# Two transformer blocks at batch 1: the first modulation columns in shift and scale pairs, with part of their sums on the tensor engine

## The chip, the core and the metric

The kernel runs on one core of one Trainium2 chip. The metric is device microseconds of one launch. Before the change three runs took 2953.93, 2954.15 and 2958.77 us; the median is 2954.15 us.

## The reference, cut to what matters

All arrays are float32. There are 256 positions and a width of 2048. A vector c modulates both norms of the first block:

```
mod = silu(c) @ w_ada + b_ada                      # w_ada 2048 x 12288
sh1, sc1, gt1, sh2, sc2, gt2 = split(mod, 6)
h = rmsnorm(x, g_mix) * (1 + sc1) + sh1
x = x + (1 + gt1) * mixer(h, w_in, w_a, w_b, w_o)  # h @ w_in comes first
h = rmsnorm(x, g_ffn) * (1 + sc2) + sh2
x = x + (1 + gt2) * conv_ffn(h, w_up, ..., w_down)
```

A second block follows: a gated convolution, then a squared-ReLU layer of width 8192. Every matrix is read once from memory, 554 MB in all. The change lies ahead of, and in the first steps of, `h @ w_in`.

## The kernel before, in words

**Pieces.** Every product against a matrix goes by pieces of 512 rows by 512 columns (1 MB). SP loads a piece into one of four `raw` buffers. ACT rounds it to `whi` (`split_hi`, L518), DVE makes the rest `wlo` (`split_lo`, L819), and both have two buffers. PE multiplies 16 blocks of it by three products each (L1310 to L1312), 48 matmuls in all (`piece`). The activations are held in two parts as well, `xh` and `xl`. A step t is one piece. ACT may write `whi` for piece t only when piece t-2 has been multiplied (`s_used`). The pieces of w_in are the steps from t = 0; four of them make one group of 512 output columns.

**The modulation.** w_ada has 24 groups of 512 columns, 4 MB each. The first 8 are sh1 (groups 0 to 3) and sc1 (groups 4 to 7) and are needed before any piece can be multiplied. SP loads each in four quarters into the buffers `ada_first`. DVE multiplies each of the 16 chunks of a group by its value of silu(c) and adds (`add_product`, L902 and L905), in two running sums (`first_sum`). PE then adds over the 128 partitions: in `modulation` (L1358) the sums are the stationary operand and a column of ones is the moving one, so a matmul has one column. A quarter's buffer is loaded anew when DVE has used its four chunks.

**The order at the start.** SP first issues 21 small vector loads, the constants and the positions, then the four quarters of group 0, then x. PE turns the vectors and x (L1383), and takes the mean of squares (`statistic`, L1349). DVE computes the rotary angles (L883 to L896), then the eight groups, then reads all eight out of PSUM at once (L921), makes `wlo` of pieces 0 and 1, the reciprocal root (`root`, L839 to L847), and normalises the 16 chunks of x (`norm_split`, L859 and L869). PE starts the pieces as soon as the first chunk is there.

**The background groups.** The other 16 groups of w_ada come in half pieces of 0.5 MB. Two buffers (`ada`) form a ring: POOL issues a load (L467) when DVE has used the half piece before the last in the same buffer. DVE takes them in `half_piece`, which stands in its program just ahead of each `split_lo`; the function `beside(t)` says how many belong to step t. They are 3 in two steps for t below 24, and some 1.1 per step after. DVE executes in order, so a half piece that has not landed holds the `split_lo` behind it. Steps from t = 24 add the attention of the mixer.

## Time and profile before

| | |
|---|---|
| profiled execution, span | 2955.1 us |
| median of the three runs | 2954.15 us |
| PE busy | 2716.0 us, 92% |
| DVE busy | 1836.5 us, 62% |
| ACT busy | 1227.9 us, 42% |
| read from memory | 553.45 MB, 188 GB/s over the span |

The profile gives the profiled execution by its span; nothing else is listed around it, and it lies 1 us above the median. PE is the busiest engine over the whole, but not in the first slices of the page, where DVE and the DMA are. So the start is read from the trace, in microseconds from its beginning.

### The profile page before, as it was taken

What the parts mean: (1) busy time and instruction counts of PE and PEld (TensorE: products, weight loads), DVE (VectorE), ACT (ScalarE), POOL (GpSimd) and SP (SyncE); (2) the same over time, 40 slices, a digit from 0 to 9 for tenths busy, and PEclk for the clock granted to TensorE, in tenths of its full rate; (3) what the DMA queues carried; (4) which work ended last, traced back from release to release, by engine and by line L of the source; (5) the groups of instructions that cost most, each with busy time, mean ns of one, the idle gap of its engine ahead of it and who ended that gap; (6) DMA issues with size and microseconds to landing.
All of it is one profiled execution on the core that took longest, in us unless ns stands there. A gap on an engine that the chain in (4) does not pass through costs nothing.

```text
span 2955.1 us, 51569 instructions
## 1 busy us (share of the span) xinstructions
PE 2716.0 (92%) x21611; PEld 2670.4 (90%) x21611; DVE 1836.5 (62%) x1881; ACT 1227.9 (42%) x1200; POOL 325.1 (11%) x364
## 2 busy tenths in 40 slices
PE   3499999999998999999999988777899999999998
PEld 3499999998998999999999977776899999999997
DVE  6966667775777555534565457999555544455444
ACT  1233643344433554432444346664443333333332
POOL 0011111100111000000000014885000000000000
PEclk8599999999999999999999999888999999999998
DMA  8888567754776455554555543332255555555552
GB/s 323 299 291 292 214 238 249 242 182 162 243 255 227 171 175 184 181 182 159 185 185 175 181 130 126 115 114 72 87 170 182 179 183 185 186 183 185 184 184 89
DMA packets 266602, 557.72 MB, mean 189 GB/s; under 512 B 11991, under 2 KB 13144, under 8 KB 266200
## 3 DMA queue, kind: packets, MB, share of 16 engines
q1 hardware_dynamic: 248023, 488.47, 48.8%
q0 software_dynamic: 18432, 67.12, 6.7%
q8 instruction: 114, 1.87, 0.3%
q14 instruction: 33, 0.26, 0.0%
HBM read 553.45 MB, written 2.10 MB: 188 GB/s over the span
## 4 chain that ended last, share of the span: by engine, by line
PE 76%; DVE 14%; issue 4%; DMA 3%; ACT 2%; SPq 1%; POOL 0%; DVEq 0%; ACTq 0%; POOLq 0%
PE ps L1310 22%; PE ps L1311 22%; PE ps L1312 22%; DVE ucv L1197 5%; DVE wlo L819 3%; DMA att<-in_w_ada 3%; DVE norm_rows L905 2%; PE ms L1312 1%; PE ms L1311 1%; PE ms L1310 1%; PE ms L1594 1%; PE ms L1349 1%; ACT whi L518 1%; PE ms L1345 1%; DMA att<-in_x 0%
## 5 line engine op out<-in xcount | busy, mean ns | idle before, releaser
L1310 PE MATMUL ps<-xh,whi 128*128 128x256 f32 x5136 | 1489.7, 290 | 113.3 <-DVE wlo L819 51.8
L819 DVE TENSOR_TENSOR wlo<-raw,whi 128x2048 fp32r<-128x2048 f32 x429 | 991.0, 2310 | 917.7 <-ACT whi L518 916.7
L1311 PE MATMUL ps<-xl,whi 128*128 128x256 f32 x5136 | 1474.3, 287 | 0.0
L1312 PE MATMUL ps<-xh,wlo 128*128 128x256 f32 x5136 | 1473.8, 287 | 0.0
L518 ACT CAST whi<-raw 128x2048 fp32r<-128x2048 f32 x429 | 816.5, 1903 | 1438.9 <-PE ps L1312 1291.3
L1310 PEld LDWEIGHTS ps<-xh,whi 128*128 128x128 f32 x5136 | 1006.8, 196 | 127.3 <-issue 71.5
L1311 PEld LDWEIGHTS ps<-xl,whi 128*128 128x128 f32 x5136 | 1006.7, 196 | 3.2 <-issue 2.9
L1312 PEld LDWEIGHTS ps<-xh,wlo 128*128 128x128 f32 x5136 | 1005.9, 196 | 0.0
L1312 PE MATMUL ps<-gh,wlo 128*128 128x256 f32 x1024 | 289.0, 282 | 0.0
L1310 PE MATMUL ps<-gh,whi 128*128 128x256 f32 x1024 | 288.9, 282 | 0.0
L1311 PE MATMUL ps<-gl,whi 128*128 128x256 f32 x1024 | 288.9, 282 | 0.0
L905 DVE SCALAR_TENSOR_TENSOR norm_rows<-att,cact,norm_rows 128x512 f32<-128x512 f32 x296 | 217.5, 749 | 60.2 <-DMA att<-in_w_ada 54.6
L1310 PEld LDWEIGHTS ps<-gh,whi 128*128 128x128 f32 x1024 | 193.2, 189 | 0.1
L1312 PEld LDWEIGHTS ps<-gh,wlo 128*128 128x128 f32 x1024 | 193.1, 189 | 0.0
L1311 PEld LDWEIGHTS ps<-gl,whi 128*128 128x128 f32 x1024 | 193.0, 188 | 0.1
L506 POOL TENSOR_TENSOR ucv<-ucv,prod 128x256 f32<-128x256 f32 x180 | 190.5, 1095 | 0.0
L467 POOL DMA_DIRECT2D att<-in_w_ada x128 | 92.8, 725 | 734.0 <-DVE norm_rows L905 520.0
L1197 DVE SCALAR_TENSOR_TENSOR ucv<-upad,cols,ucv 128x256 f32<-128x256 f32 x240 | 173.4, 794 | 0.0
L489 POOL TENSOR_TENSOR prod<-sq 128x256 f32<-128x256 f32 x24 | 20.7, 874 | 996.3 <-ACT sq L528 979.7
L721 ACT ACTIVATE prod<-upad,cols 128x256 f32<-128x256 f32 x180 | 87.0, 505 | 55.3 <-POOL ucv L506 53.0
L1310 PE MATMUL ps<-fh,whi 128*128 (+1 forms) x352 | 99.4, 282 | 3.5 <-DVE cb L1149 3.5
L1312 PE MATMUL ms<-fh,wlo 128*128 (+1 forms) x352 | 99.9, 284 | 0.0
(230 smaller groups left out, 2059.0 us busy)
## 6 DMA issues: line engine op xcount, KB each, us to landing
raw<-in_w_in SPq DMA_DIRECT2D x88, 1024.0 KB, 5.3
raw<-in_w_up SPq DMA_DIRECT2D x88, 1024.0 KB, 4.8
att<-in_w_ada POOLq DMA_DIRECT2D x128, 512.0 KB, 4.9
raw<-in_ffn_w_up SPq DMA_DIRECT2D x64, 1024.0 KB, 5.1
raw<-in_ffn_w_down SPq DMA_DIRECT2D x64, 1024.0 KB, 5.1
raw<-in_conv_w_pw SPq DMA_DIRECT2D x48, 1024.0 KB, 5.3
raw<-in_w_down SPq DMA_DIRECT2D x44, 1024.0 KB, 5.1
att<-in_w_ada SPq DMA_DIRECT2D x32, 1024.0 KB, 7.2
```

The costliest lines, as they stand in the source:

```text
L467: pool.dma_start(slots[m % 2][:, :, :], w_ada[m % 8][:, :, n:n + NCOL]).then_inc(s_adaland[m % 2], 16)
L506: nc.gpsimd.tensor_tensor(dst, dst, src, ALU.add).then_inc(s_padd, 1)
L518: nc.scalar.copy(whi[t % SPL][:, :, :], raw[t % RAW][:, :, :]).then_inc(s_hi, 1)
L721: nc.scalar.activation(dst, src, ACT.Copy, scale=w).then_inc(s_prod, 1)
L819: nc.vector.tensor_tensor(wlo[t % SPL][:, :, :], raw[t % RAW][:, :, :], whi[t % SPL][:, :, :].bitcast(F32), ALU.subtract).then_inc(s_lo, 1)
L905: ins = nc.vector.scalar_tensor_tensor(sums, w, cx, sums, ALU.mult, ALU.add)
L1197: nc.vector.scalar_tensor_tensor(ucv[:, c, :], src, w, ucv[:, c, :], ALU.mult, ALU.add).then_inc(s_dwd, 1)
L1310: mm(o, h, rh, start=start, stop=False, skip_group_check=True)
L1311: mm(o, h, rl, start=False, stop=False, skip_group_check=True)
L1312: return mm(o, l, rh, start=False, stop=stop, skip_group_check=True)
L1345: mm(o, mean_w[:, :], pair_sum(k, i), start=i == 0, stop=i == 7).then_inc(s_psum, 1)
L1349: ins = mm(o, mean_w[:, :], sq[:, 2 * (i % 2) + m, :], start=i == 0 and m == 0, stop=i == 7 and m == 1)
```

## The change

**Loads.** SP issues the constants, only the first three vectors (b_ada, c, g_mix), then group 0 and at once pieces 0 and 1 of w_in. Pieces 2 and 3 follow the third and fifth group. The other vectors, the positions and x are issued by ACT, ahead of its own work.

**Pairs.** The eight groups are taken in the order 0, 4, 1, 5, 2, 6, 3, 7 (`FIRST`), so that each pair gives shift and scale of four chunks of x. After a pair DVE normalises those four chunks (`norm_first`) and PE multiplies one piece of w_in with them.

**Sums.** Of a group's 16 chunks DVE does 10 (`first_products`). PE does the other 6: the chunk of w_ada is the stationary operand and silu(c) the moving one, 24 matmuls of one column (`first_modulation`), and then 8 more over DVE's two sums. The quarters 2 and 3 are reloaded only when PE has used them too.

**Background.** The angles move into the steps t = 4 to 12. The ring of half pieces starts after the last pair is normalised, and its first 36 half pieces belong to the steps 3 to 23 in place of 0 to 23. Steps 0 to 3 are now inside the loop over pairs.

```diff
+FIRST = [j + 4 * half for j in range(4) for half in range(2)]
+BY_VECTOR = 10
+BY_TENSOR = KC - BY_VECTOR // KC
+B_ANGLE = 4
...
-            return 3 * t // 2
+            return 36 * max(0, t - 3) // 21
...
-        first_sum = [mod_sum, [tCDE[:, 0:NCOL], tCDE[:, NCOL:2 * NCOL]]]
+        first_sum = [[ch(26, 28), ch(28, 30)], [tCDE[:, 0:NCOL], tCDE[:, NCOL:2 * NCOL]]]
...
+        first_vecs = [v for v in vec_parts if v[3] < P]
+        other_vecs = [v for v in vec_parts if v[3] >= P]
...
+            load_vectors(sp, first_vecs, s_vin[0])
...
+            for n, group in enumerate(FIRST):
                 for q in range(KC):
-                    sp.wait_ge(s_chain, g * DC + KC * (q + 1))
-                    sp.dma_start(ada_first[q][:, :, :], w_ada[q][:, :, bass.ds(g * NCOL, NCOL)]).then_inc(s_adaring[q], 16)
+                    if n:
+                        if KC * q < BY_VECTOR:
+                            sp.wait_ge(s_first, BY_VECTOR * (n - 1) + min(BY_VECTOR, KC * (q + 1)))
+                        if KC * (q + 1) > BY_VECTOR:
+                            sp.wait_ge(s_firstmm, BY_TENSOR * (n - 1) + q + 1 - (KC - BY_TENSOR))
+                    sp.dma_start(ada_first[q][:, :, :], w_ada[q][:, :, group * NCOL:(group + 1) * NCOL]).then_inc(s_adaring[q], 16)
+                for q in {0: (0, 1), 2: (2,), 4: (3,)}.get(n, ()):
+                    sp.dma_start(raw[q][:, :, :], blocks("w_in")[q][:, :, 0:NCOL]).then_inc(s_land[q], 16)
...
+            load_vectors(act, other_vecs, s_vin[1])
+            act.dma_start(posi, A["positions"]).then_inc(s_in[1], 16)
+            x_in = A["x"].rearrange("b (c p) (h t) -> p (b c) h t", p=P, t=T)
+            for c in range(2):
+                act.dma_start(att[:, 8 * c:8 * c + 8, :], x_in[:, c]).then_inc(s_in[2], 16)
+            act.wait_ge(s_trc, 1)
...
-            norm_hi(0, lambda c: mod[:, c:c + 1])
+            for j in range(4):
+                for c in range(4 * j, 4 * j + 4):
+                    act.wait_ge(s_nt, c + 1)
+                    nc.scalar.activation(xh[:, c, :], sq[:, c % 4, :], ACT.Identity, bias=mod[:, c:c + 1]).then_inc(s_nh, 1)
+                if j < 2:
+                    split_hi(0, 2 + j)
...
+            def first_products(n):
+                dve.wait_ge(s_gemv, n + 1)
+                for kc in range(BY_VECTOR):
+                    if kc % KC == 0:
+                        dve.wait_ge(s_adaring[kc // KC], 16 * (n + 1))
+                    sums, cx = first_sum[n % 2][kc % 2], cact[:, kc:kc + 1]
+                    w = ada_first[kc // KC][:, kc % KC, :]
+                    if kc < 2:
+                        nc.vector.tensor_scalar(sums, w, cx, None, ALU.mult).then_inc(s_first, 1)
+                    else:
+                        dve.wait_ge(s_first, BY_VECTOR * n + kc - 1)
+                        nc.vector.scalar_tensor_tensor(sums, w, cx, sums, ALU.mult, ALU.add).then_inc(s_first, 1)
+            def read_first(n):
+                a = FIRST[n]
+                c = slice(4 * a, 4 * a + 4)
+                dve.wait_ge(s_gemv, 2 + n + 1)
+                nc.vector.tensor_tensor(mod[:, c], first_bank[n % 2][:, c], cols[:, AT["b_ada"] + 4 * a:AT["b_ada"] + 4 * a + 4], ALU.add).then_inc(s_firstmod, 1)
...
+            def norm_first(j):
+                c0 = 4 * j
+                dve.wait_ge(s_firstmod, 2 * j + 2)
+                sv.did(nc.vector.scalar_tensor_tensor(gmod[:, 0, c0:c0 + 4], mod[:, DC + c0:DC + c0 + 4], 1.0, cols[:, AT["g_mix"] + c0:AT["g_mix"] + c0 + 4],
+                                                      ALU.add, ALU.mult))
+                sv.wait()
+                if j:
+                    dve.wait_ge(s_h, c0)
+                for c in range(c0, c0 + 4):
+                    nc.vector.scalar_tensor_tensor(sq[:, c % 4, :], res[:, c, :], gmod[:, 0, c:c + 1], rstd[:, :], ALU.mult, ALU.mult).then_inc(s_nt, 1)
+                for c in range(c0, c0 + 4):
+                    dve.wait_ge(s_nt, c + 1)
+                    dve.wait_ge(s_nh, c + 1)
+                    nc.vector.scalar_tensor_tensor(xl[:, c, :], sq[:, c % 4, :], mod[:, c:c + 1], xh[:, c, :].bitcast(F32),
+                                                   ALU.add, ALU.subtract).then_inc(s_h, 1)
...
-            with dve.Fori(0, ADA_START // 2) as i:
-                for par in range(2):
-                    dve.wait_ge(s_gemv, i * 2 + (par + 1))
-                    for q in range(KC):
-                        dve.wait_ge(s_adaring[q], i * 32 + (16 * par + 16))
-                        for c in range(KC):
-                            kc = KC * q + c
-                            add_product(first_sum[par][c % 2], ada_first[q][:, c, :], kc, i * 32, DC * (1 + par) + kc, back=2)
-            dve.wait_ge(s_sin, 4)
-            for n in range(2):
-                sv.did(nc.vector.tensor_scalar(rope[:, 2 * n + 1, :], rope[:, 2 * n + 1, :], cons[:, C_SIGN + n:C_SIGN + n + 1], None, ALU.mult))
-            read_modulation(0, ADA_START)
-            dve.wait_ge(s_mod, 1)
-            sv.did(nc.vector.scalar_tensor_tensor(gmod[:, 0, :], mod[:, DC:2 * DC], 1.0, cols[:, AT["g_mix"]:AT["g_mix"] + DC],
-                                                  ALU.add, ALU.mult))
-            split_lo(0, 0)
-            split_lo(0, 1)
-            root(0, EPS1)
-            norm_split(0, 0, H_QKV, lambda c: gmod[:, 0, c:c + 1], lambda c: mod[:, c:c + 1])
+            for n in range(ADA_START):
+                first_products(n)
+                if n == 0:
+                    dve.wait_ge(s_in[1], 16)
+                    nc.vector.tensor_copy(posf, posi).then_inc(s_posf, 1)
+                if n:
+                    read_first(n - 1)
+                if n == 1:
+                    split_lo(0, 0)
+                    split_lo(0, 1)
+                    root(0, EPS1)
+                if n and n % 2 == 0:
+                    norm_first(n // 2 - 1)
+                    if n < 6:
+                        split_lo(0, n // 2 + 1)
+            read_first(ADA_START - 1)
+            norm_first(3)
+            dve.sem_inc(s_chain, DC * (1 + ADA_START))
...
+            def first_modulation(n):
+                bank, a = first_bank[n % 2], 4 * FIRST[n]
+                if n >= 2:
+                    pe.wait_ge(s_firstmod, n - 1)
+                for kc in range(BY_VECTOR, DC):
+                    if kc == BY_VECTOR or kc % KC == 0:
+                        pe.wait_ge(s_adaring[kc // KC], 16 * (n + 1))
+                    for m in range(4):
+                        ins = mm(bank[:, a + m:a + m + 1], ada_first[kc // KC][:, kc % KC, P * m:P * (m + 1)], cact[:, kc:kc + 1],
+                                 start=kc == BY_VECTOR and m == 0, stop=False, skip_group_check=True)
+                    if kc % KC == KC - 1:
+                        ins.then_inc(s_firstmm, 1)
+                pe.wait_ge(s_first, BY_VECTOR * (n + 1))
+                for m in range(4):
+                    for x in first_sum[n % 2]:
+                        ins = mm(bank[:, a + m:a + m + 1], x[:, P * m:P * (m + 1)], ones[:, 0:1], start=False, stop=x is first_sum[n % 2][-1], skip_group_check=True)
+                ins.then_inc(s_gemv, 1)
...
+            pe.wait_ge(s_in[0], 16)
+            pe.wait_ge(s_vin[0], 16 * len(first_vecs))
+            turned(0, [att[:, 16, 0:P]])
+            pe.wait_ge(s_cact, 1)
+            pe.wait_ge(s_const, 4)
+            first_modulation(0)
+            pe.wait_ge(s_vin[1], 16 * len(other_vecs))
+            for b in range(1, 3):
+                if b == 2:
+                    pe.wait_ge(s_trc, 1)
+                turned(b, [att[:, 17 + 4 * (b - 1) + i, 0:P] for i in range(4)])
+            pe.wait_ge(s_posf, 1)
+            mm(bank_o[:, T:2 * T], ones[0:1, :], posf, start=True, stop=True).then_inc(s_posb, 1)
+            pe.wait_ge(s_in[2], 32)
+            for b in range(3, 3 + DC // 2):
+                if b < 5:
+                    pe.wait_ge(s_trc, b - 1)
+                else:
+                    pe.wait_ge(s_trx, b - 4)
+                turned(b, [att[:, 8 * c + m // 2, (m % 2) * P:(m % 2 + 1) * P] for m in range(2 * (b - 3), 2 * (b - 3) + 2) for c in range(2)])
             statistic(0)
-
-            with pe.Fori(0, ADA_START // 2) as i:
-                for par in range(2):
-                    modulation(i * 2, par, first_sum[par])
-            pe.wait_ge(s_mod, 1)
+            first_modulation(1)
+            for n in range(2, ADA_START):
+                first_modulation(n)
+                if n % 2 == 0:
+                    if n == 2:
+                        pe.wait_ge(s_free[0], 1)
+                    piece(0, n // 2 - 1, ps[0], lambda c: from_x(2 * n - 4 + c), n == 2, False, H_QKV + 2 * n - 4)
+            piece(0, 3, ps[0], lambda c: from_x(12 + c), False, True, H_QKV + 12)
+            pe.wait_ge(s_firstmod, ADA_START)
```

On PE, before: after the transposes of x and the squares come the one-column matmuls over DVE's sums, eight for a group, four rows of two (a row of the loop over the groups is printed once). `norm_rows` and `tCDE` hold the running sums, `ms` is PSUM.

```order
L1349 MATMUL ms<-sq,mean_w 128x256 x16
L1388 UNCONDITIONAL_BRANCH
L1388 ISA
L1358 ISA
L1358 MATMUL ms<-ones,norm_rows 128x1 x2
```

And in the changed kernel, from the program's start to the first piece: `att` holds the quarters of w_ada, `cact` is silu(c), L1439 is `first_modulation`'s part on w_ada and L1446 the part on DVE's sums.

```order
L1453 MATMUL ms<-cons,att 128x128
L1439 MATMUL ms<-cact,att 128x1 x24
L1446 MATMUL ms<-ones,att 128x1 x8
L1453 MATMUL ms<-cons,att 128x128 x8
L1468 MATMUL ms<-att,ones 128x256
L1453 MATMUL ms<-cons,att 128x128 x32
L1419 MATMUL ms<-sq,mean_w 128x256 x16
L1439 MATMUL ps<-cact,att 128x1 x24
L1446 MATMUL ps<-ones,tCDE 128x1 x8
```

So a group has 32 matmuls of one column where it had 8, and the first group's stand ahead of the transposes of x.

On DVE, before: from the end of the loop over the groups to the normalised x. All eight groups are read at once, and two splits stand between them and the root.

```order
L934 TENSOR_SCALAR rope<-rope,cons 128x256
L921 TENSOR_TENSOR mod<-ms,cols 128x32 [waits modulation_group_summed]
L937 SCALAR_TENSOR_TENSOR gmod<-mod,cols 128x16 [waits modulation_read_out]
L819 TENSOR_TENSOR wlo<-raw,whi 128x2048 [waits piece_hi_made] x2
L839 TENSOR_SCALAR norm_rows<-ms 128x256 [waits squares_used]
L841 RECIPROCAL norm_rows<-norm_rows 128x256 [waits root_made]
```

In the changed kernel, DVE after the products of the third group (the first of the second pair): it reads a group out, normalises four chunks, makes `wlo` of piece 2, and only then begins the fourth group.

```order
L954 SCALAR_TENSOR_TENSOR att<-att,cact 128x512 [waits first_modulation_product_added]
L961 TENSOR_TENSOR mod<-ps,cols 128x4 [waits modulation_group_summed]
L982 SCALAR_TENSOR_TENSOR gmod<-mod,cols 128x4 [waits first_modulation_read_out]
L988 SCALAR_TENSOR_TENSOR sq<-res,gmod,norm_rows 128x256 [waits vector_step]
L988 SCALAR_TENSOR_TENSOR sq<-res,gmod,norm_rows 128x256 x3
L992 SCALAR_TENSOR_TENSOR xl<-sq,mod,xh 128x256 [waits normed_chunk_hi,normed_chunk_scaled] x4
L847 TENSOR_TENSOR wlo<-raw,whi 128x2048 [waits piece_hi_made]
L951 TENSOR_SCALAR tCDE<-att,cact 128x512 [waits first_modulation_landed0,modulation_group_summed]
```

The split of piece 2 (and after the fifth group that of piece 3) stands between the groups and waits for ACT's half, which waits for `s_used`.

## Rows read from the trace of the kernel before

**Rows 1.** Chain of waits, 0 to 260 us: start, us, what
```profile
95.66 7.26 DMA att<-in_w_ada
111.21 3.59 PE ms L1358 x16
```

**Rows 2.** The same chain, 205 to 245 us
```profile
216.18 7.34 DMA att<-in_w_ada
```

**Rows 3.** Timeline 0 to 63 us: start, us, engine, line, tiles, count, idle before
```profile
0.75 1.28 ACT L553 ACT_TABLE_LOAD   x1 [0.75 <-PEq L1645]
11.09 0.42 SPq L384 DMA_DIRECT2D cons<-in_consts  x1
...
14.46 4.74 SPq L395 DMA_DIRECT2D att<-in_x  x2
...
18.16 0.22 ACT L553 ACTIVATE cact<-cols 128x16 f32<-128x16 f32 x1 [16.12 <-DVE cols L876]
48.03 1.84 PE L1358 MATMUL ms<-ones,norm_rows 128*128 128x1 f32 x16
49.73 1.93 PE L1358 MATMUL ms<-ones,tCDE 128*128 128x1 f32 x16
50.01 0.88 DVE L902 TENSOR_SCALAR norm_rows<-att,cact 128x512 f32<-128x512 f32 x2 [4.48 <-PE ms L1358]
50.81 9.36 DVE L905 SCALAR_TENSOR_TENSOR norm_rows<-att,cact,norm_rows 128x512 f32<-128x512 f32 x14
```

**Rows 4.** Windows: span, then busy (count) of PE, PEld, DVE, ACT, POOL; PEclk; DMA; GB/s
```profile
32.30:38.30 6.00, 6.00 (x27) 5.06 (x28) 6.00 (x11) 3.33 (x6) 0.00 (x0) 1.00 1.05 408
48.10:52.00 3.90, 3.56 (x33) 3.47 (x31) 1.99 (x4) 0.13 (x1) 0.00 (x0) 1.00 0.84 319
52.10:60.00 7.90, 0.00 (x0) 0.00 (x0) 7.90 (x13) 0.00 (x0) 0.00 (x0) 0.50 0.86 305
60.30:63.90 3.60, 3.57 (x16) 3.49 (x16) 3.60 (x7) 0.00 (x0) 0.00 (x0) 0.50 1.04 399
125.40:130.50 5.10, 5.08 (x24) 5.10 (x25) 5.10 (x14) 3.12 (x8) 0.00 (x0) 0.50 0.06 23
```

**Rows 5.** DMA issues, windows 52.3:52.9 and 137.8:138.6: KB each, us to landing
```profile
att<-in_w_ada SPq DMA_DIRECT2D x1, 1024.0 KB, 5.0
att<-in_w_ada POOLq DMA_DIRECT2D x1, 512.0 KB, 3.9
```

**Rows 6.** Timeline: first full read-out, root, first chunk, first piece
```profile
114.82 0.19 DVE L921 TENSOR_TENSOR mod<-ms,cols 128x32 f32<-128x32 f32 x1 [3.22 <-PE ms L1358]
119.54 0.42 DVE L839 TENSOR_SCALAR norm_rows<-ms 128x256 f32<-128x256 f32 x1
123.61 1.28 DVE L859 SCALAR_TENSOR_TENSOR sq<-res,gmod,norm_rows 128x256 f32<-128x256 f32 x3
125.42 0.55 PE L1310 MATMUL ps<-xh,whi 128*128 128x256 f32 x1 [10.64 <-DVE xl L869]
```

**Rows 7.** Timeline: pieces t = 2, 3, 4 and 23 begin; the ring begins
```profile
136.28 0.49 DVE L902 TENSOR_SCALAR norm_rows<-att,cact 128x512 f32<-128x512 f32 x1
145.61 0.58 PE L1310 MATMUL ps<-xh,whi 128*128 128x256 f32 x1 [6.19 <-DVE wlo L819]
153.83 0.28 PE L1310 MATMUL ps<-xh,whi 128*128 128x256 f32 x1
159.59 0.28 PE L1310 MATMUL ps<-xh,whi 128*128 128x256 f32 x1
276.26 0.28 PE L1310 MATMUL ps<-xh,whi 128*128 128x256 f32 x1
```

**Rows 8.** DVE groups of lines, 159.6 to 276.3 us: count, busy, mean ns, idle
```profile
L819 DVE TENSOR_TENSOR wlo<-raw,whi 128x2048 fp32r<-128x2048 f32 x19 | 43.4, 2285 | 1.3 <-ACT whi L518 1.3
L905 DVE SCALAR_TENSOR_TENSOR norm_rows<-att,cact,norm_rows 128x512 f32<-128x512 f32 x54 | 40.5, 751 | 27.5 <-DMA att<-in_w_ada 26.5
L902 DVE TENSOR_SCALAR norm_rows<-att,cact 128x512 f32<-128x512 f32 x4 | 1.9, 484 | 4.9 <-DMA att<-in_w_ada 4.9
```

More of the change, by code:

```diff
@@ L261, in build @@
         s_in = [sem(f"input_landed{i}") for i in range(3)]
-        s_vin = sem("vectors_landed")
+        s_vin = [sem(f"vectors{i}_landed") for i in range(2)]
+        s_first = sem("first_modulation_product_added")
+        s_firstmm = sem("first_modulation_product_multiplied")
+        s_firstmod = sem("first_modulation_read_out")
         s_const = sem("constants_made")
@@ L370, in build, with load_vectors @@
                 done += n
+        first_vecs = [v for v in vec_parts if v[3] < P]
+        other_vecs = [v for v in vec_parts if v[3] >= P]
+        def load_vectors(eng, parts, landed):
+            for name, done, n, at in parts:
+                v = A[name]
+                letters = "abc"[:len(v.shape)]
+                flat = v.rearrange(f"{' '.join(letters)} -> ({' '.join(letters)})") if len(v.shape) > 1 else v
+                eng.dma_start(att[at % P:at % P + n, 16 + at // P, 0:P],
+                              flat.rearrange("(r p) -> r p", p=P)[done:done + n, :]).then_inc(landed, 16)
+        first_bank = (bank_m, ps[1][:, 0:2, :].rearrange("p a t -> p (a t)"))
         block = ctx.enter_context(nc.Block())
@@ L419, in _ @@
             w_in = blocks("w_in")
-            columns(0, 14, w_in, 0, KC)
+            columns(0, 14, w_in, 0, KC, start=1)
             sp.wait_ge(s_lo, T_SMALL + 1)
@@ L573, in background @@
             def background(t):
+                if t == B_ANGLE + 5:
+                    act.wait_ge(s_ang, 1)
+                    for n in range(2):
+                        nc.scalar.activation(rope[:, 2 * n, :], rB[:, T * n:T * (n + 1)], ACT.Sin).then_inc(s_sin, 1)
+                        nc.scalar.activation(rope[:, 2 * n + 1, :], rA[:, T * n:T * (n + 1)], ACT.Sin).then_inc(s_sin, 1)
                 if B_VTA <= t < B_VTA + 4 or B_VTB <= t < B_VTB + 4:
@@ L624, in background @@
                     nc.scalar.copy(att[:, 24 + h - 2, :], bank_o[:, 0:T]).then_inc(s_obc, 1)
-            for t in range(1, T_WAB + 1):
+            for t in range(3, T_WAB + 1):
                 split_hi(0, t + 1)
@@ new lines, in angles @@
+            def angles(step):
+                if step == 0:
+                    dve.wait_ge(s_posb, 1)
+                    for n in range(2):
+                        sv.did(nc.vector.tensor_scalar(rA[:, T * n:T * (n + 1)], bank_o[:, T:2 * T], cons[:, C_FREQ + n:C_FREQ + n + 1], None, ALU.mult))
+                if step == 1:
+                    sv.wait()
+                    sv.did(nc.vector.tensor_scalar(rB, rA, 1.0 / TWO_PI, ROUND, ALU.mult, ALU.add))
+                    sv.wait()
+                    sv.did(nc.vector.tensor_scalar(rB, rB, ROUND, None, ALU.subtract))
+                if 2 <= step < 4:
+                    for part in TWO_PI_PARTS[:2] if step == 2 else TWO_PI_PARTS[2:]:
+                        sv.wait()
+                        sv.did(nc.vector.scalar_tensor_tensor(rA, rB, -part, rA, ALU.mult, ALU.add))
+                if step == 3:
+                    sv.wait()
+                    sv.did(nc.vector.tensor_scalar(rA, rA, PI_IN, -PI_IN, ALU.min, ALU.max))
+                if step == 4:
+                    sv.wait()
+                    sv.did(nc.vector.scalar_tensor_tensor(rB, rA, -1.0, rA, ALU.mult, ALU.min))
+                    sv.wait()
+                    nc.vector.tensor_scalar(rB, rB, HALF_PI, None, ALU.add).then_inc(s_ang, 1)
+                if step == 8:
+                    dve.wait_ge(s_sin, 4)
+                    for n in range(2):
+                        sv.did(nc.vector.tensor_scalar(rope[:, 2 * n + 1, :], rope[:, 2 * n + 1, :], cons[:, C_SIGN + n:C_SIGN + n + 1], None, ALU.mult))
@@ L972, in background @@
             def background(t):
+                angles(t - B_ANGLE)
                 h = (t - B_STICK) // 2
@@ L1065, in background @@
                     nc.vector.tensor_copy(tA[:, 0:384], bank_f[:, 0:384]).then_inc(s_ptc, 1)
-            for m in beside(0):
-                half_piece(m)
-            for t in range(1, T_WAB + 1):
+            for t in range(3, T_WAB + 1):
                 background_first(t)
@@ L1500, in attend @@
                 last_mm[0] = mm(bank_o[:, P:T], att[:, v, P:T], w[:, T:384], start=False, stop=True)
-            for t in range(T_WAB):
+            for t in range(KC, T_WAB):
                 if t == B_STICK:
```

100 lines of the change are left out of this document (23 added, 77 removed).

## The prediction

> **What bounds the kernel now.** I read the page's slices first: PE is busy nearly everywhere except at the start, where DVE and the DMA are. So I followed the chain of waits through the first 260 us [rows 1]. From DVE's sums and the loads of w_ada, which hold each other (7.3 us for a load at 95.7), it goes to PE's sums at 111.2. In the second stretch of the chain [rows 2] a load of half a MB takes 7.3 us again and again: the ring of background half pieces sets the pace of the steps 4 to 23, and not PE. The groups of DVE's lines [rows 8] say it by sums: in 116.7 us DVE made 19 splits and 58 products, which is 29 half pieces, one per 4.02 us, and it sat idle 32 us for landings. PE's own pace is 5.76 us a piece (153.83 to 159.59 [rows 7]), but t = 4 to t = 23 took 116.7 us for 19 pieces, 6.14 each. From t = 24 the ring has only 1.1 half pieces per step and PE sets the pace, so I take a shift at t = 23 to arrive whole at the end. The sum therefore asks one thing: when does t = 23 begin (before: 276.26 [rows 7]).
>
> **The price of a one-column matmul.** Eight of them are 16 records. They took 1.84 and 1.93 us at full granted clock [rows 3], and 3.57 us at half [rows 4]; that is 0.118 and 0.223 us a record. The change gives a group 32 of them, 64 records: 16 on quarter 2, 32 on quarter 3, 16 on DVE's sums. That is 3.6 + 7.1 + 3.6 = 14.3 us at half clock and 1.9 + 3.8 + 1.9 = 7.6 us at full. Before, a group cost DVE 10.2 us (0.88 + 9.36 [rows 3]) and PE 3.6 beside it.
>
> **Which clock.** PE had made the squares' means when it came to 48.1 to 52.0, where it ran only one-column sums with hardly a pause (3.56 of 3.90 us) at full granted clock. Right behind, from 52.1, it was half [rows 4]. The later bursts of sums were all at half, and so were the first 5.1 us of pieces (125.4 to 130.5). At t = 2 too, the first piece after a pause took 8.2 us and the next 5.76 [rows 7]. I read this so: one-column matmuls neither raise the clock nor hold it; pieces and the squares' matmuls do. (The column shows 1.00 from the start, before PE had done anything, so I read nothing from it there.) I let a pass that follows a piece run full for 3.5 us, which is an estimate from the 3.9 us of the window 48.1 to 52.0, and the rest at half.
>
> The Trainium skill, page "TensorE: Matmul & The Clock Gate", section "Why this matters for your kernels", says that keeping TensorE continuously busy gets the full clock. By that rule the passes, which keep PE busy, would run at full; that is the first rival below. The row of 48.1 to 52.0 speaks against it.
>
> **Up to the first pass (kernel time in us).** ACT now issues 22 loads before anything else. SP took 22 issues in 0.76 to 11.09, 0.47 each [rows 3]; no row shows ACT issuing one. Bounds: 0.3 each, and some 4 us more in all, as for the two issues of x, which kept SP 4.74; I take 0.47, the nearest kind of row. So silu(c) is at 0.75 + 10.3 + 1.28 (table) + 0.22 = 12.6, against 18.16. w_ada starts at 2.6 in place of 11.9; a MB takes 2.57 us at 408 GB/s [rows 4]. I take quarter 2 at 13.7 and quarter 3 at 19, since the vectors and x share the engines.
> The Trainium skill, page "DMA: Bandwidth & Descriptors", says of the SP and ACT queues that they are not engines of their own: the second queue saves issue time and brings no bandwidth. The sum agrees: x and the vectors are counted against w_ada.
> Pass 0 at half clock: 13.7 + 3.6, then 19 + 7.1 + 3.6 = 29.7. Behind it on PE stand the other vectors, positions, x and squares: 2.8 (eight transposes at 0.22 each, 6.0 us for 27 [rows 4], and the positions, an estimate) + 15.9 (32.3 to 48.1) = 18.7, so pass 1 starts at 48.4, though its data have long landed. It takes 3.5 us full and 34.5 records at half, 11.2 us: 59.6. Pass 2: 14.3, so 73.9. DVE's part is ready: its splits wait for ACT's squares, the root ends near 57 (4.0 us [rows 6]), its ten products take 6.3 (0.88 + 8 of 0.67), norm 4: 67.
>
> **Piece 0 and the new wait.** Piece 0 starts cold, 8.2 us [rows 7]: 82.1. ACT may only now write `whi` for piece 2 (1.9 + 0.1), and DVE's `split_lo` (2.3), which stands ahead of the fourth group's products, ends at 86.4. Queued behind this wait are all of DVE's products, and behind these SP's loads of w_ada: the DMA falls idle.
>
> **One full turn (groups 3 and 4, piece 1).** From the end of that split: SP issues quarter 0 of group 4 after four products (0.88 + 2 of 0.67, and 0.15 to issue), and it lands 5.0 later [rows 5]: +7.35; quarters 2 and 3 land at +12.5 and +15.1. PE's pass 4: 12.5 + 3.6 + 7.1 + 3.6 = 26.8, piece 8.2 = 35.0, ACT and DVE 4.3 = 39.3. So the fourth split ends at 125.7. Two groups took 20.5 us before (10.2 each). At full clock the turn is 15.1 + 3.8 + 1.9 + 5.8 + 4.3 = 31.
>
> **To the ring.** Groups 5 and 6 with piece 2: +35.0 = 160.7. Pass 7: 11.2 = 171.9. Read-out and gain 0.5, four chunks 4.0 (from the 0.8 us a chunk at 123.6 to 125.4 and the tail; bounds 3 to 5) = 176.4; POOL issues 0.3 later and half a MB lands in 3.9 alone [rows 5]: 180.6. There DVE begins the ring, where before it began at 136.28, with both buffers full. Its split of piece 4 ends at 180.6 + 1.5 + 2.3 and PE begins t = 4 at 184.4, 24.8 later than before.
>
> **The ring.** It has 34 half pieces before the split of t = 23, as before, so its pace counts, not the steps. A buffer's turn is 0.3 (POOL) + landing + 1.5 (two products). Bounds: PE's pace, 5.8 us a step or 3.4 a half piece, and the 4.02 above [rows 8]. With fewer splits between half pieces (6 of 21 steps have a single one, before every second) I take 3.8, nearer the row. t = 23 begins at 180.6 + 33 x 3.8 + 1.5 + 2.3 = 309.8: 33.5 later. The angles (about 6 us of DVE in t = 4 to 12) lie in DVE's idle 32 us; without it they would cost 1 us a step.
>
> **The sum.** 2955.1 + 33.5 = 2988.6 us, less the 1 us by which the profile stands above the median: 2987.6 us. The pieces that move ahead are in it: they are worth 4 x 5.8 us of PE, and PE's 384 added one-column records (eight times 48) are what eats them.
>
> **Rivals.**
> 1. The one-column passes count and the clock stays full. For it: PE is busy by the engine row; against it the fall at 52. Then: pass 0 ends 24.7, pass 1 51.0, DVE's products gate pass 2 at 61.1, third split 71.7, fourth 102.7, piece 2 at 129.3, pass 7 136.9, ring at 145.7, t = 23 at 275.0: 1.3 earlier, 2952. With the ring at 4.02 it is 2959: no change to be told.
> 2. The other side, faster: the queue of w_ada sets the pace. All that is loaded up to the last quarter is 41.0 MB (33.6 w_ada, 4.2 w_in, 2.1 x, 1.2 small), 100.6 us at 408 GB/s, from 3: 104. Then 3.8 + 1.9 + 0.5 + 4.0 + 0.3 + 3.9: ring at 118.5, t = 23 at 247.8, 28.5 earlier: 2926. It decides from the point where PE's 128 records and a piece fit in the 20.6 us of eight quarters (0.116 us a record, so full clock) and DVE's splits of pieces 2 and 3 do not hold up the next group's loads. For it: the DMA is at 1.04 there now. Against it: both conditions.
> 3. The passes are slow, but the ring keeps PE's pace: t = 4 at 184.4 and 19 x 5.83 = 295.2, 18.9 later: 2973. For it: a half piece alone lands in 3.9. Against it: a piece and 1.71 half pieces in 5.8 us are 1.95 MB, 335 GB/s, where the ring waited at 1.84 MB in 6.14, 299.
>
> **How the numbers follow.** Forecast 0.70, rival 3 0.13, rival 1 0.10, rival 2 0.07. The forecast's own range is 2974 to 3003: the ring's bounds of 3.6 and 4.02 (7 down and 7 up), ACT's issues (4 up), the clock's moment in four places (6 either way). The range of 8 in 10 is 2958 to 3006: it takes in rival 3 and the slow edge of rival 1 and leaves out the rest of 1, rival 2 and a tail above. A change of 0.2%, 5.9 us, is about what can be told. Faster 0.09 (rival 2 and a part of 1), same 0.09 (1), slower 0.82.
>
> **What would show it.** Right: one-column records near 0.22 us in most passes and half clock there; PE nearly without idle time from 14 to 170; DVE waiting for ACT's half of pieces 2 and 3 near 67 to 84 and again 35 to 39 us later; DMA under half busy between the pairs; first piece near 74, t = 4 near 184, ring 3.7 to 3.9 us a half piece. Wrong: records at 0.12 us behind one-column work alone; t = 4 before 165; or steps from t = 24 that take back what was lost.

## The result, and the profile after

The changed kernel takes 2992.88 us (median of 4 runs, 2987.67 to 2995.94), the kernel before 2954.04 beside it (4 runs, 2951.68 to 2958.77). The ratio is 1.0127, 95% interval 1.0113 to 1.0141: slower by 1.3%, 38.8 us. The profiled execution took 2992.79 us, its span is 2991.0.

The chain of waits of the changed kernel, up to the ring (start us, us, what):

```profile
4.19 19.13 DMA att<-in_w_ada
23.37 6.98 PE ms L1439 x32
30.35 3.41 PE ms L1446 x16
...
44.28 7.73 PE ms L1419 x32
52.01 8.05 PE ps L1439 x48
60.06 3.41 PE ps L1446 x16
63.47 10.24 PE ms L1439 x48
73.71 3.41 PE ms L1446 x16
...
95.34 7.57 DMA att<-in_w_ada
103.04 10.37 PE ms L1439 x48
113.41 3.41 PE ms L1446 x16
...
171.50 3.43 PE ps L1446 x16
175.35 1.08 DVE sq L988 x3
178.03 4.05 DMA att<-in_w_ada
182.17 0.50 DVE norm_rows L936
```

Where loads and DVE's sums held each other before [rows 1], TensorE's one-column passes now stand in the chain (a pass is PE's work on one group: 48 records on w_ada and 16 on DVE's sums), 13.7 us each (10.24 + 3.41), and the ring begins at 182.17, where it began at 136.28 [rows 7]. The timeline of the same kernel shows silu(c), the pieces t = 0, 1, 4 and 23, and DVE's splits of pieces 2 and 3 between them (start, us, engine, line, tiles, count, idle before):

```profile
13.79 0.21 ACT L573 ACTIVATE cact<-cols 128x16 f32<-128x16 f32 x1
76.99 0.56 PE L1380 MATMUL ps<-xh,whi 128*128 128x256 f32 x1
86.93 2.29 DVE L847 TENSOR_TENSOR wlo<-raw,whi 128x2048 fp32r<-128x2048 f32 x1 [16.06 <-ACT whi L533]
116.69 0.56 PE L1380 MATMUL ps<-xh,whi 128*128 128x256 f32 x1
127.17 2.29 DVE L847 TENSOR_TENSOR wlo<-raw,whi 128x2048 fp32r<-128x2048 f32 x1 [19.27 <-ACT whi L533]
186.11 0.28 PE L1380 MATMUL ps<-xh,whi 128*128 128x256 f32 x1
309.38 0.39 PE L1380 MATMUL ps<-xh,whi 128*128 128x256 f32 x1 [0.74 <-DVE wlo L847]
```

Twice DVE stood idle for 16 and 19 us with the next group's products behind it. The windows (columns as in [rows 4]) are: pass 2 with its sums; the end of piece 0; the 3.3 us behind it; the 3.5 us behind those; a whole turn, from piece 0 to piece 1; the ring with t = 4 to 23.

```profile
63.30:77.00 13.70, 13.70 (x66) 13.70 (x66) 7.50 (x17) 1.70 (x4) 0.00 (x0) 0.50 1.02 383
81.40:84.90 3.50, 3.50 (x32) 3.50 (x31) 0.00 (x0) 0.00 (x0) 0.00 (x0) 1.00 0.00 0
84.90:88.20 3.30, 3.30 (x33) 3.30 (x31) 1.27 (x1) 1.90 (x1) 0.00 (x0) 1.00 0.03 7
88.30:91.80 3.50, 3.50 (x17) 3.44 (x17) 3.50 (x6) 0.00 (x0) 0.00 (x0) 0.50 0.00 0
77.00:116.70 39.70, 32.06 (x178) 31.91 (x178) 18.31 (x32) 3.60 (x5) 0.00 (x0) 0.59 0.65 239
186.10:309.40 123.30, 115.45 (x947) 113.60 (x945) 94.66 (x97) 44.06 (x30) 23.84 (x33) 1.00 0.89 301
```

PE was busy for all of 13.7 us of one-column work and its clock stayed at half. It rose in piece 0 and fell 3.3 us behind it. In the 3.3 us at full PE made 33 records of the next pass, in the 3.5 us at half 17. Over a turn the DMA moves 239 GB/s; 408 were to be had [rows 4].

DVE's groups of lines while the ring feeds t = 4 to 23, against [rows 8]:

```profile
L939 DVE SCALAR_TENSOR_TENSOR norm_rows<-att,cact,norm_rows 128x512 f32<-128x512 f32 x62 | 46.6, 751 | 26.2 <-DMA att<-in_w_ada 24.6
L847 DVE TENSOR_TENSOR wlo<-raw,whi 128x2048 fp32r<-128x2048 f32 x19 | 43.4, 2284 | 0.0
```

Of the 38.8 us, 33.1 are there when t = 23 begins (309.38 against 276.26 [rows 7]). Steps 23 to 72 add nothing: the split of piece 72 begins 32.9 us later than before (640.89 against 608.03). Another 3.6 appear behind it, where the two kernels run the same instructions: from that split to the last one 2317.2 us against 2313.7. The remaining 2.3 are not in the two profiles, whose spans are 35.9 us apart, but in the medians. Over all 14 kernels profiled here the stretch behind the split of piece 72 took 2312.8 to 2319.0, with no order in it that I can name, so up to 6 us of one kernel's difference from another may be this. For that reason each run below is also read at t = 23.

### The profile page after: what moved, and what is told of

Same layout as the page of the kernel before. It is cut to its first block, busy times and chain, and to the rows that moved or that the text cites. A ratio compares the mean times of both kernels' runs of the same rounds, so it can differ in the third digit from the quotient of the medians.

```text
span 2991.0 us, 52038 instructions
## 1 busy us (share of the span) xinstructions
PE 2794.4 (93%) x21995; PEld 2747.7 (92%) x21995; DVE 1806.1 (60%) x1841; ACT 1229.2 (41%) x1203; POOL 325.1 (11%) x364
## 4 chain that ended last, share of the span: by engine, by line
PE 75%; DVE 13%; DMA 6%; issue 3%; ACT 2%; POOL 0%; SPq 0%; DVEq 0%; ACTq 0%; POOLq 0%
PE ps L1380 21%; PE ps L1381 21%; PE ps L1382 21%; DMA att<-in_w_ada 6%; DVE ucv L1267 5%; DVE wlo L847 3%; DVE norm_rows L939 2%; PE ms L1382 1%; PE ms L1380 1%; PE ms L1381 1%; PE ms L1439 1%; ACT whi L533 1%; PE ms L1688 1%; PE ms L1419 1%; PE ms L1415 1%
## 5 line engine op out<-in xcount | busy, mean ns | idle before, releaser
L939 DVE SCALAR_TENSOR_TENSOR norm_rows<-att,cact,norm_rows 128x512 f32<-128x512 f32 x240 | 180.0, 750 | 54.9 <-DMA att<-in_w_ada 49.3
L1382 PE MATMUL ps<-fh,wlo 128*128 (+1 forms) x352 | 100.4, 285 | 0.0
```

Source lines behind the costliest of these rows:

```text
L939: ins = nc.vector.scalar_tensor_tensor(sums, w, cx, sums, ALU.mult, ALU.add)
L1382: return mm(o, l, rh, start=False, stop=stop, skip_group_check=True)
```

## The experiments

Twelve kernels ran. All but the control start from the changed kernel ("after"). Each was timed against the kernel before on the same chip (medians there 2956.92, 2955.59 and 2956.14 us in the three sittings; the changed kernel had 2954.04 beside it, so differences of medians across sittings carry 2 to 3 us). The expectations say TensorE for PE, VectorE for DVE and ScalarE for ACT. The middle columns are from the profiles (the kernel before: t = 4 at 159.6, t = 23 at 276.3); a turn is from piece 0 to piece 1 and from piece 1 to piece 2.

| run | turns | t = 4 | t = 23 | median us | ratio to before |
|---|---|---|---|---|---|
| after | 39.7, 39.9 | 186.1 | 309.4 | 2992.9 | 1.0127 (1.0113 to 1.0141) |
| vec16 | 35.3, 36.3 | 166.8 | 293.1 | 2979.1 | 1.0069 (1.0046 to 1.0092) |
| wide64 | 39.3, 39.4 | 176.4 | 302.2 | 2982.1 | 1.0083 (1.0061 to 1.0105) |
| late | 31.8, 31.7 | 165.7 | 290.7 | 2973.7 | 1.0057 (1.0036 to 1.0079) |
| even | 39.3, 40.0 | 184.0 | 297.0 | 2982.2 | 1.0084 (1.0063 to 1.0106) |
| early | 38.8, 39.6 | 181.5 | 303.8 | 2984.8 | 1.0100 (1.0083 to 1.0117) |
| wide128 | 32.5, 33.4 | 153.0 | 276.9 | 2959.7 | 1.0019 (1.0009 to 1.0029) |
| wide128_late | 23.8, 23.1 | 134.7 | 257.7 | 2941.6 | 0.9953 (0.9936 to 0.9969) |
| vec14_late | 23.8, 23.8 | 140.7 | 267.7 | 2951.2 | 0.9981 (0.9971 to 0.9990) |
| vec14_all | 25.1, 24.6 | 140.7 | 254.4 | 2941.3 | 0.9958 (0.9941 to 0.9974) |
| start14 | 24.6, 24.3 | 130.2 | 242.9 | 2931.4 | 0.9918 (0.9901 to 0.9934) |
| start12w | 24.9, 23.6 | 127.5 | 239.8 | 2928.0 | 0.9904 (0.9887 to 0.9920) |
| before_even | - | 152.9 | 265.0 | 2954.5 | 0.9996 (0.9986 to 1.0005) |

The start is not quite the same even where the instructions are. In all that leads up to piece 0, after, even, late and early are one program, but the clock fell in pass 1 at 54.06, 55.02, 56.23 and 56.28 us, and piece 0 began at 76.99, 75.71, 73.10 and 73.64. The first parts of pass 1 in after and in early:

```profile
51.85 8.21 PE L1439 MATMUL ps<-cact,att 128*128 128x1 f32 x48
```

```profile
51.15 5.56 PE L1439 MATMUL ps<-cact,att 128*128 128x1 f32 x48
```

So 1.3 to 3.9 us of what even, late and early gain on after were there before their edits acted.

### Is it TensorE's share of the sums? (vec16)

```diff
-BY_VECTOR = 10
+BY_VECTOR = 16
```

> The changed kernel, but DVE does all 16 chunks of a first group; PE is left with 8 one-column matmuls a group. My theory (the one-column passes at half clock fill PE, and the splits of pieces 2 and 3 hold DVE): PE's part of a group falls from 14.2 us to 3.6, DVE's rises from 6.3 to 10.2; the turn from the second split to the next falls from 40 us to about 37, the last two groups are bound by DVE, the ring begins near 168 in place of 182, and the time is about 2979. Rival (the passes cost nothing that counts, the held loads do): 2993 or more, since DVE now has 4 us more a group. Faster than before (under 2948) would mean that the wait for the splits doesn't matter either.

2979.1 us, the number expected, though the ring began at 163.17 and not near 168, and 3.6 of the 16.3 us won at t = 23 were lost again by the split of piece 72: 14 us of the loss go with TensorE's share, and 25 stay. The turns are still 35.3 and 36.3 us although PE is busy for only 14.2 us of the first, because DVE now has 16 chunks a group and still waits for ACT's half of piece 2 (9.3 us) and of piece 3 (10.2 us). So TensorE's passes are only one part of the loop.

### Is it the clock? (wide64, wide128)

```diff
-ins = mm(bank[:, a + m:a + m + 1], ada_first[..][.., P * m:P * (m + 1)], cact[:, kc:kc + 1],
+ins = mm(bank[:, 256 + 64 * m:256 + 64 * m + 64], ada_first[..][.., P * m:P * (m + 1)], cact[:, kc:kc + 64],
...
-    ins = mm(bank[:, a + m:a + m + 1], x[:, P * m:P * (m + 1)], ones[:, 0:1],
+    ins = mm(bank[:, 256 + 64 * m:256 + 64 * m + 64], x[:, P * m:P * (m + 1)], ones[:, 0:64],
```

The weights loaded are the same; only the first column of each result is used.

> The changed kernel with the moving operand of the first groups' passes 64 columns wide in place of one; the extra columns are zeros (ones in the last eight matmuls) and land in unused PSUM columns. The same 64 weight loads a group. My theory (the clock is half because one-column matmuls don't count as work for it): the granted clock is full in the passes, a record takes 0.12 to 0.16 us in place of 0.22 although it does more, a group's pass 8 to 10 us, and the time falls to 2960 to 2978. Rival 1 (these matmuls are slow by themselves, whatever the clock): records at 0.22 or more, 2993 or slower. Rival 2 (width beyond one is not what the clock looks at): half clock, records 0.22, 2993 to 3000.

> As wide64 with 128 columns in place of 64 in each matmul of the passes (all but the first column of each are left unused; the vector after a chunk's own is read from its neighbours and zeros). With 64 columns the passes held the full clock for longer than one-column passes do, but a pass that began at half clock stayed there to its end (10.47 for 48 records). Theory (the amount streamed counts against weight loading, so more columns also raise the clock): passes 4 and 6 begin at half clock and rise within 10 us, records fall from 0.22 to 0.12 to 0.16, time 2960 to 2978. Rival 1 (128 columns hold but never raise it, as 64): passes 4 and 6 at 0.22 a record or more, time 2979 to 2984. Rival 2: the streaming itself becomes the bound, records of 0.25 to 0.45 at half clock: passes 12 to 22, time 2990 to 3030.

The timeline of wide64 and its window of pass 4, which begins at half clock:

```profile
97.82 10.47 PE L1440 MATMUL ms<-cact,att 128*128 128x64 f32 x48 [3.81 <-DMA att<-in_w_ada]
118.24 5.47 PE L1440 MATMUL ps<-cact,att 128*128 128x64 f32 x48
```

```profile
97.90:108.20 10.30, 10.30 (x49) 10.30 (x49) 4.71 (x12) 1.71 (x4) 0.00 (x0) 0.50 1.05 405
```

And of wide128, pass 6, which begins at half clock too, with the windows of its two parts:

```profile
119.07 8.35 PE L1440 MATMUL ms<-cact,att 128*128 128x128 f32 x48 [3.30 <-DMA att<-in_w_ada]
```

```profile
119.10:124.80 5.70, 5.70 (x27) 5.70 (x28) 5.37 (x14) 1.71 (x4) 0.00 (x0) 0.50 1.05 409
124.90:127.30 2.40, 2.40 (x24) 2.40 (x23) 2.14 (x4) 0.00 (x0) 0.00 (x0) 1.00 1.05 403
```

All three kinds of pass keep PE without a gap. With 64 columns a pass that comes from a piece at full clock stays there (5.47 us for 48 records, where one column took 6.4 to 7.6), but one that begins at half ends at half (10.47). With 128, and the same weight loads, the clock rises within the pass: 27 records in 5.7 us, then 24 in 2.4. My theory for wide64 said 2960 to 2978 and failed at 2982.1; for wide128 it held, and the time (2959.7) was 0.3 us below its range. 128 columns cost a record nothing that shows: 5.5 us for 48 at full clock, as with 64. So the slow clock is worth 33 us of this kernel: piece 0 begins 14.0 us earlier than in after, the two turns are 13.7 us shorter, and the stretch from piece 2 to t = 4 is 5.5 shorter.

### Is it DVE's order? (late)

```diff
-                    if n < 6:
-                        split_lo(0, n // 2 + 1)
+                if n in (3, 5):
+                    split_lo(0, (n + 1) // 2)
```

The splits of pieces 2 and 3 now stand behind the products of their time and not ahead of them.

> The changed kernel with the splits of pieces 2 and 3 made by DVE one group later (behind the products of the fourth and sixth group), so that its wait for ACT's half no longer holds products and loads. My theory (PE's passes are the bound, and the held DVE costs only the idle time that PE has between them, 7 to 8 us in each of two turns): the ring begins near 168, 2978. Rival (the hold is what costs, 16 and 19 us of DVE): 2958 or less. Third: nothing changes, because the loads wait for PE anyway: 2993.

2973.7. DVE still waits for ACT's half, here 6.67 us and in the next turn 10.29, but the fourth group's products, which release the next loads, are done ahead of it:

```profile
82.70 2.29 DVE L847 TENSOR_TENSOR wlo<-raw,whi 128x2048 fp32r<-128x2048 f32 x1 [6.67 <-ACT whi L533]
```

The window of a turn shows what is left then:

```profile
73.10:104.90 31.80, 31.80 (x177) 31.80 (x178) 21.16 (x37) 3.60 (x5) 0.00 (x0) 0.61 0.85 309
```

PE is busy for the whole turn, at a mean clock of 0.61: in after it idled 7.6 us of 39.7, now it is the bound. The passes are as slow as they were (10.38 us). It is 4 us better than I had expected, and the ring began at 162.09, not near 168. Of this, 3.9 us are the start: piece 0 began at 73.10 and not at 76.99. What the edit itself gives is the two turns, 7.9 and 8.2 us, as the theory said.

### Both (wide128_late, vec14_late)

> Both cures of the turn together: passes of 128 columns (which rose to full clock within a pass; alone 2959.7) and the splits of pieces 2 and 3 behind the products of their time (alone 2973.7), VectorE still at 10 chunks. Theory (two links of one loop: at half clock TensorE's 32 us a turn is the bound and VectorE's order hides behind it, at full clock VectorE's held turn of 32.5 to 33.4 is): with both, TensorE needs 2 x 7.5 + 6 = 21, VectorE 2 x 7.5 + 8 = 23, the loads 26 a turn. So 26, t=4 from 153.0 in wide128 to 138 to 142, 2944 to 2950. Rival (either cure alone already removes what can be had, another wait sets 32): 2957 to 2961.

> The splits of pieces 2 and 3 stand behind the products of their time, as in the run late, and VectorE makes 14 of the 16 chunks of a group (10 in after), TensorE two. Theory (the turn is now TensorE's, back to back at half clock: two passes of 10.38 + 3.55 and a piece of 8 us less overlaps, 31.8 in late): a pass shrinks to 16 records of 0.22 = 3.5, so TensorE needs 2 x 7.1 + 8 = 22 a turn, VectorE 2 x 14 x 0.64 = 18 and its splits, squares and norms, some 25, and the loads (two groups of 4 MB and a piece of 2 MB at some 400 GB/s) 25 to 26. The turn falls from 31.8 to 26, three turns bring t=4 from 165.7 to 148, t=23 from 290.7 to 273, and the time from 2973.7 to 2956 (range 2952 to 2964). Rival: passes of any length at half clock are not what sets the turn, something with each group's hand-over does (the gain was only VectorE's order): turn 30 to 32 and a time of 2970 or more.

The two cures add: late took 19.2 us off, wide128 33.2, both 51.3. (3.9 of late's 19.2 are the start; in the turns alone late saves 16.1 us, wide128 13.7, both 32.8.) In after the two losses stand one behind the other, not side by side: DVE waits for the piece, the piece for the passes, the passes for the loads that DVE's products release. Turns of wide128_late, vec14_all and start12w:

```profile
87.60:110.70 23.10, 20.56 (x180) 20.21 (x178) 20.60 (x37) 3.61 (x5) 0.00 (x0) 1.00 1.05 407
```

```profile
94.70:119.30 24.60, 18.47 (x114) 18.36 (x114) 23.38 (x42) 3.60 (x5) 0.00 (x0) 0.64 0.96 348
```

```profile
82.70:106.40 23.70, 18.64 (x148) 18.30 (x146) 21.64 (x38) 3.60 (x5) 0.00 (x0) 0.93 1.03 380
```

In wide128_late the DMA moves 407 GB/s through the turn: the queue of w_ada is the bound, which was my second rival's condition, and the time falls below the kernel before. vec14_late (14 chunks on DVE, 16 records on w_ada in a pass, in every second pass at half clock) comes to nearly the same turn without the full clock; in vec14_all's turn above DVE is busy for 23.38 of 24.60 us, so DVE and the loads are both near their end. Both kernels came out below the range I had given, vec14_late at 2951.2 (2952 to 2964) and wide128_late at 2941.6 (2944 to 2950). I had expected turns of 26 us in both and got 23.1 to 23.8, since I had counted 2 MB for a piece of w_in and it is 1: eight quarters and a piece are 9.44 MB, 23.1 us at 408 GB/s.

### The ring (even, early, before_even)

```diff
-            return 36 * max(0, t - 3) // 21
+            return 88 * max(0, t - 3) // 69
-            return 36 + (t - 24) * 13 // 12
+            return 88 * (t - 3) // 69
```

Both kernels with the even ring also read the second batch of modulation columns four steps later, since their half pieces come later (so do vec14_all, start14 and start12w); "nothing else" below leaves this out.

> The changed kernel with the 88 background half pieces spread evenly over the steps 3 to 71 (1.28 a step) in place of 36 ahead of step 24 (1.71 a step). My theory (the ring and not PE sets the pace of the steps 4 to 23): these 19 pieces take about 112 us in place of 123, nothing of it is lost later or at most 3 us, and the time is 2981 to 2985. Rival (a shift or a gain there is taken back after step 24, since DVE has more to do in the later steps): 2990 to 2996.

> The kernel before with the 88 half pieces spread evenly over its first 72 steps and nothing else. A control for even: if the even ring is worth its 10.8 us by itself, the kernel before gains too: 19 pieces of 116.7 us (159.59 to 276.26) at 6.0 each make 114, t=23 at 273, so about 3 to 6 us: 2948 to 2951. Rival: no gain, as the ring before already keeps TensorE's pace (6.14 a piece): 2953 to 2957.

Windows of even, from t = 4 to 23 and from the split of piece 24 to that of piece 40, and of after in the second stretch:

```profile
184.00:297.00 113.00, 112.43 (x938) 112.23 (x937) 83.60 (x81) 43.37 (x29) 17.78 (x25) 1.00 0.87 294
299.20:423.70 124.50, 117.62 (x970) 116.08 (x968) 86.61 (x99) 76.33 (x80) 21.31 (x27) 1.00 0.64 220
```

```profile
313.80:431.30 117.50, 113.39 (x940) 112.45 (x939) 81.33 (x92) 73.59 (x77) 19.12 (x24) 1.00 0.64 226
```

Spread evenly, 19 pieces took 113.0 us (5.95 each) and not 123.3, but the sixteen steps from 24 on took 7.0 us more. At the split of piece 72 even is 6.2 us ahead of after, of which 2.1 were there at t = 4; 3.8 more of its 10.7 us stand in the tail that differs among all kernels. The control says the same: before_even is 10.4 us ahead of before at the split of piece 23 (262.01 against 272.43), 3.8 at that of piece 72, and 1.1 in the median, within the interval, since its tail took 3.1 us more. The theory for it (2948 to 2951) failed. The rival's range held, but not its reason: the even ring did take 4.6 us off the 19 pieces from t = 4 on, and 6.7 ahead of them. A gain read at t = 23 is thus not always whole at the end, as I had taken it in expecting 2981 to 2985 for the right number and the wrong reason; a shift of the ring's start was whole in after (32.9 of 33.1), but not in vec16 (12.7 of 16.3).

```diff
-            norm_first(3)
             dve.sem_inc(s_chain, DC * (1 + ADA_START))
+            norm_first(3)
```

> after with one change: the ring of later w_ada loads is released by VectorE ahead of the last normalisation and not behind it (the normalisation of piece 3 took 3.4 us and waited for TensorE's last pass). Theory: the ring is behind the matmuls from t=4 on, so its start moves by some 4 us and t=23 with it: 2989. Rival: the ring's first loads compete with nothing and only wait for their own products on VectorE, which stand behind the normalisation in its order anyhow: no more than 1 us, 2991 to 2993.

2984.8, 8 us less than after, more than either theory. From DVE's last read-out to the ring's first product it is 4.5 us (170.35 to 174.82) in place of 7.2 (174.96 to 182.17): there the edit is worth 2.7. Another 4.6 were there ahead of it: the clock happened to stay full to 56.28 and not to 54.06, piece 0 began at 73.64, 3.35 us earlier, and the turns were 1.3 shorter. But t = 4 also begins only 4.6 us earlier (181.5), because PE is at piece 3 until then, and t = 23 5.6 (303.8). So of the edit's 2.7 us 1.0 is left at t = 23, which is what the rival said, and 0.3 at the split of piece 72; 3.6 more of the 8 us are in the tail. The time tells nothing of the edit.

### What beats both kernels (vec14_all, start14, start12w)

vec14_all is vec14_late with even and early. start14 changes the order at the start too: ACT's and DVE's splits of pieces 0 and 1 move to DVE's idle time near 28 us, TensorE's pass 1 ahead of the mean square, DVE's third group ahead of the root. start12w is start14 with 128 columns and 12 chunks on DVE.

```diff
-                if n:
-                    read_first(n - 1)
-                if n == 1:
                     split_lo(0, 0)
                     split_lo(0, 1)
+                if n:
+                    read_first(n - 1)
+                if n == 2:
                     root(0, EPS1)
...
-            statistic(0)
             first_modulation(1)
+            statistic(0)
```

> vec14_late, and the ring's 88 half pieces spread evenly over the steps t=3 to 71, and the ring released before the last normalisation and not behind it. Theory (each part does what it did alone): even took 12.4 off t=23 against after and 10.8 off the time, the earlier release should give 4. From 2956 for vec14_late to 2941 to 2945, t=23 near 258: below the kernel before. Rival 1: with the pieces done earlier, the ring is no longer behind its matmuls in the same way, the two gains overlap and t=23 stays at 268 or more, 2951 or more. Rival 2: the evenly spread ring takes back in steps 24 to 71 what it gave before: in even that was 12.4 - 10.8 = 1.6 us.

> vec14_all (2941.3) with a changed order in the first 60 us alone: ScalarE's and VectorE's splits of pieces 0 and 1 move from behind the squares into the idle time at 26 to 30 us, TensorE's pass 1 goes ahead of the mean square and VectorE's products of group 2 ahead of the root. Theory (the loads stop at 45.6 to 49.9 and 57.5 to 59.5 because quarters are held by engines that do other work first, and every load not sent there is missing at t=3): the first piece from 69.6 to about 60, the loads run on, t=4 from 140.7 to 130 to 134 and the time to 2931 to 2936. Rival 1 (VectorE with 7 groups x 10.4 + splits + norms, some 95 us from 30, is then the bound): t=4 at 134 to 137, 2936 to 2939. Rival 2 (what is gained at the start is lost before t=3, as the passes are still at half clock): 2939 to 2942.

> start14 with the passes of 128 columns and 12 chunks on VectorE in place of 14. Theory: with the full clock a pass is 32 records of 0.115 and sums of 1.95, 5.6 in all, TensorE's turn 17 to 18 and VectorE's 2 x 9.0 + 8 = 26; the loads are then the only bound, and the last group of w_ada lands some 5 us earlier than with 14: t=4 at 126 to 130, 2926 to 2932. Rival: the loads already set the pace of start14: within 2 us of it.

start12w's window from the landing of the first group to the first piece, and of start14 the same:

```profile
22.60:57.80 35.20, 32.37 (x219) 28.71 (x219) 25.59 (x40) 17.61 (x27) 0.00 (x0) 1.00 1.05 406
```

```profile
23.90:60.00 36.10, 32.32 (x171) 27.74 (x171) 29.85 (x47) 18.05 (x27) 0.00 (x0) 0.92 1.04 396
```

(The clock's column counts 1.00 where the profile has no record of it, here up to 27.7 and 37.3 us.) All three came out inside the range of their theory: 2941.3, 2931.4 and 2928.0. vec14_all's t = 23 came at 254.4 and not near 258; but of the 15.4 us by which it is ahead of vec14_late at the split of piece 23, 8.2 are left at that of piece 72, as in even. With the new order the loads never stop before the first piece; in vec14_all they ran at a mean of 304 GB/s from 22.4 to 69.6 us. The 3.5 us between the last two are too few to be told apart by these intervals. start12w is 28.2 us faster than the kernel before and 64.9 faster than the changed one, with the changed kernel's own idea (early loads, pairs of columns, pieces among the passes) in it.

## Why the prediction was right

The forecast was slower, 2987.6 us (range 2958 to 3006); it came out at 2992.9. By its steps:

- **Clock and price of a pass.** Right. 64 records were priced at 14.3 us at half clock and took 13.9 (10.38 + 3.55, read in the timeline). A pass behind a piece was to run full for 3.5 us: 3.3 in pass 3. Rival 1 (by its own terms 2953 and 2960, not 2952 and 2959) fell with this, and wide128 shows that it was the clock: with the same weight loads at full clock 33 us came back. But the rows of before did not decide this, and here the premise was better than its evidence. The fall at 52 that I set against rival 1 came when PE had stood idle since 51.66 (49.73 + 1.93 [rows 3], and no record from 52.1 to 60.0 [rows 4]); so it fits the idle time as well as the one-column work. The later bursts of one column followed idle time and lasted 3.6 us, while pieces too ran at half for their first 5.1 us. The first row that tells the two apart is the pass of 13.7 us above. The full stretch behind a piece was 3.3, 4.0 and 2.7 us, but only 2.1 behind the squares, one of the four places that I had given 6 us for.
- **The start.** silu(c) was to be done at 12.6 and was done at 14.00: ACT's 22 issues lasted to 12.5, 0.53 us each and not 0.47. Quarters 2 and 3 were to land at 13.7 and 19 and landed at 16.17 and 23.32. Beside group 0's 4.2 MB the DMA had moved 4.0 MB by then: 2.6 of x and vectors, 0.66 of constants, which I had not counted, and 0.6 of pieces 0 and 1. Pass 0 ended 4.1 later (33.8), and pass 1, root and piece 0 followed 3 to 4 us late (51.85, 61.1, 76.99).
- **The wait of DVE.** Right in place and size: the third split ended at 89.2 (forecast 86.4), the fourth 40.2 later (39.3), piece 2 ended at 164.0 (160.7). late and vec16 show that it is one of two causes and not a consequence of the slow passes alone. One of my signs was read wrongly: PE "nearly without idle time" was true from 23.4 to 85 us, but not before, where PE waited 3.5 us for quarter 3; the turn that I had worked out has idle time in it, while quarters 2 and 3 load, and so it was (7.6 us).
- **Ring.** It began 1.6 us later than forecast, 182.17 against 180.6: pass 7 ended 3.0 late (174.9 against 171.9), but reading out, gain and normalisation behind it took 3.1 us (174.9 to 178.0) and not 4.5. Its pace was 3.74 us a half piece (307.04 - 182.17 - 1.5, by 33), forecast 3.8, so rival 3 (PE's pace) fell. t = 23: 309.38 against 309.8. That the two agree within 0.4 us is luck: errors of 1 to 4 us had cancelled, the late end of pass 7 against a shorter normalisation and a faster ring.
- **What I missed** is behind t = 23: I carried the 33.5 to the end unchanged, and the medians say 38.8. Of the 5.3 us between, 3.6 lie in the tail, which I had taken as the same in every kernel; the rest is within the medians' spread (2987.67 to 2995.94).
- **Rival 2**, the queue of w_ada as the pace, was rightly refused for this kernel, for the two conditions that I named. wide128_late meets both and lands at 2941.6, not at 2926: its ring begins at 131.04 and not at 118.5, as its first piece starts only at 63.85 and the loads still had idle time ahead of it. start12w, with the new order at the start, 12 chunks on DVE and the even and early ring, begins it at 123.02.

## What to carry to other kernels

Price a matrix-vector product on TensorE at the clock it will have, not at the one of the matmuls around it; here one-column passes ran at half clock with the engine busy throughout, and 127 unused columns cost less than the slow clock. When work for several engines is interleaved by hand, look for the operation that waits on the far end of the loop and put it behind what feeds the loads; and read a turn's window with the DMA's GB/s in it, since here the turn reached its least, 23.1 us, when that column read 407.

## What the runs showed of the hardware

- Passes of one column ran into half clock 2.7 to 4.0 us behind a piece and stayed there. Passes of 64 columns behind a piece stayed at full (5.47 us for 48 records), from half they stayed at half (10.47). Passes of 128 columns rose. The Trainium skill, page "TensorE: Matmul & The Clock Gate", section "Why this matters for your kernels", speaks of keeping the engine continuously busy; here that was not enough, with 13.7 us without a gap at half clock.
- With fp32 operands and loaded weights a record cost the same for 1, 64 and 128 columns at full clock (1.93, 1.95 and 1.95 us for sixteen). That loading the weights sets it fits the rows, where PEld is as busy as PE (13.70 of 13.70), but no run shows it by itself.
- The moment at which the clock falls is not the same from kernel to kernel in the same instructions (54.06 in after, 56.28 in early); pass 1's first part took 8.21 us in the one and 5.56 in the other, and piece 0 began 3.35 us apart.
- The same instructions from the split of piece 72 to the end took 2312.8 to 2319.0 us in the 14 kernels profiled. What decides it stays open.
